# A two-layer hybrid decoder trunk on one core: scores of both attention branches in one matmul for the first two query tiles, one mask product for all heads of a step, and a new table of woven-in pieces

## What is computed

```python
def hybrid_layer(...):
    h = rmsnorm(x, g)
    z = h @ w_in
    ...
    o_cmp, p_cmp = cmp_attention(q, compress(heads(kc), pos_k, kw1, kw2), compress(heads(vc), pos_v, vw1, vw2))
    idx, ok = selection_indices(p_cmp, S)
    q_rot = apply_rope(q, cos, sin)
    o_slc = slc_attention(q_rot, apply_rope(heads(ks), cos, sin), heads(vs), idx, ok)
    o_win = win_attention(q_rot, apply_rope(heads(kwn), cos, sin), heads(vwn))
    gates = jax.nn.sigmoid(gate_logits.astype(F32)).reshape(B, S, N_HEADS, 3)
    y_nsa = (gates[..., 0:1] * o_cmp + gates[..., 1:2] * o_slc + gates[..., 2:3] * o_win).reshape(B, S, D_NSA)
    ...
    return x + y @ w_out
```

## Time and profile before

| | |
|---|---|
| median of 3 runs | 574.74 us (573.56 to 575.91) |
| the profiled execution's own time | 574.41 us |
| its span, first to last instruction | 572.6 us |
| PE busy | 547.0 us (96%) |
| DVE busy | 395.9 us (69%) |
| ACT busy | 291.9 us (51%) |
| POOL busy | 43.7 us (8%) |
| mean granted TensorE clock | 0.991 |
| bytes moved | 49.94 MB, mean 87 GB/s |

### The profile page before, as it was taken

The page is one execution under the profiler, slowest core; times in us unless marked ns, Lnnn a source line. Parts: engine busy times, 40 slices in busy tenths (PEclk is TensorE's granted clock), DMA queues, the critical chain, the costliest instruction groups (busy, mean ns, idle before and its releaser), DMA issues.

```text
span 572.6 us, 8894 instructions
## 1 busy us (share of the span) xinstructions
PE 547.0 (96%) x3327; PEld 409.8 (72%) x3327; DVE 395.9 (69%) x652; ACT 291.9 (51%) x584; POOL 43.7 (8%) x86
## 2 busy tenths in 40 slices
PE   4999999998999999999999999999899999999994
PEld 3777867777877766676887687777787777667763
DVE  4776996686866786765656679668877667676542
ACT  3647545623565554452543673562456545455431
POOL 3001100220000000000340110013000000000000
PEclk9999999998999999999999999999999999999998
DMA  9648465365111110111423756627321122000112
GB/s 260 180 146 215 114 160 107 88 135 138 38 38 38 38 37 1 38 38 38 109 76 94 182 133 164 129 62 148 98 68 38 40 73 73 1 1 2 38 37 74
DMA packets 92042, 49.94 MB, mean 87 GB/s; under 512 B 40912, under 2 KB 90208, under 8 KB 92000
## 3 DMA queue, kind: packets, MB, share of 16 engines
q1 hardware_dynamic: 89376, 45.17, 31.0%
q0 software_dynamic: 1536, 3.15, 2.3%
q10 hardware_dynamic: 1088, 1.06, 0.6%
HBM read 44.12 MB, written 2.10 MB: 81 GB/s over the span
## 4 chain that ended last, share of the span: by engine, by line
PE 80%; DVE 10%; issue 4%; ACT 3%; DMA 2%; POOL 0%; POOLq 0%; DVEq 0%; ACTq 0%
PE z_ps L1444 13%; PE z_ps L1446 12%; PE z_ps L1445 12%; PE s_ps L1516 7%; PE t_ps L1538 7%; PE o_ps L1574 5%; PE a_ps L1574 4%; PE o_ps L1444 3%; PE o_ps L1446 3%; PE o_ps L1445 3%; DVE w_lo L1072 2%; PE s_ps L1522 2%; PE t_ps L1543 1%; PE t_ps L1548 1%; PE t_ps L1635 1%
## 5 line engine op out<-in xcount | busy, mean ns | idle before, releaser
L1444 PE MATMUL z_ps<-h_hi,w_hi 128*128 128x512 f32 x248 | 102.1, 412 | 3.1 <-DVE h_lo L1056 2.3
L1008 ACT ACTIVATE probs<-s_ps,mn 128x128 f32<-128x128 f32 (+3 forms) x128 | 66.6, 523 | 74.6 <-DVE mn L1346 72.9
L1446 PE MATMUL z_ps<-h_hi,w_lo 128*128 128x512 f32 x248 | 97.8, 394 | 0.0
L1445 PE MATMUL z_ps<-h_lo,w_hi 128*128 128x512 f32 x248 | 97.8, 394 | 0.0
L866 ACT ACTIVATE w_hi<-stage 128x1024 fp32r<-128x1024 f32 x56 | 58.9, 1054 | 60.2 <-PE z_ps L1446 36.5
L1346 DVE TENSOR_REDUCE mn<-s_ps 128x1 f32<-128x384 f32 (+3 forms) x88 | 52.4, 637 | 50.2 <-PE s_ps L1522 50.0
L1072 DVE TENSOR_TENSOR w_lo<-stage,w_hi 128x1024 fp32r<-128x1024 f32 x56 | 68.4, 1221 | 10.6 <-ACT w_hi L866 9.8
L1444 PEld LDWEIGHTS z_ps<-h_hi,w_hi 128*128 128x128 f32 x248 | 47.3, 191 | 16.5 <-issue 6.6
L1446 PEld LDWEIGHTS z_ps<-h_hi,w_lo 128*128 128x128 f32 x248 | 47.1, 190 | 10.4
L1445 PEld LDWEIGHTS z_ps<-h_lo,w_hi 128*128 128x128 f32 x248 | 47.3, 191 | 8.7 <-issue 0.2
L1516 PE MATMUL s_ps<-k_st,q_st 64*128 64x128 f32 (+3 forms) x384 | 46.7, 356 | 0.2
(11 more groups left out here) (228 smaller groups left out, 915.3 us busy)
## 6 DMA issues: line engine op xcount, KB each, us to landing
stage<-in_w_in SPq DMA_DIRECT2D x28, 512.0 KB, 4.2
stage<-in_w_in SPq DMA_DIRECT2D x32, 256.0 KB, 3.8
stage<-in_cmp_k_w SPq DMA_DIRECT2D x8, 512.0 KB, 3.8
stage<-in_cmp_v_w SPq DMA_DIRECT2D x8, 512.0 KB, 5.0
stage<-in_w_out SPq DMA_DIRECT2D x8, 512.0 KB, 3.5
stage<-in_w_out SPq DMA_DIRECT2D x16, 256.0 KB, 3.9
swp<-E POOLq DMA_DIRECT2D x48, 64.0 KB, 2.3
out<-xT SPq DMA_DIRECT2D x8, 256.0 KB, 2.8
```

Of the source, the lines that this page charges most:

```text
L1008: act.activation(probs[:, 4 * pair + 2 * g + r, c0:c0 + W], s_ps[g][:, at * W:(at + 1) * W], ACT.Exp, scale=-1.0, bias=mn[:, m % 2, g, at: ...
L1444: pe.matmul(bank, w_hi[:, slot, at:at + P], x_hi, start=first, stop=False)
L1445: pe.matmul(bank, w_hi[:, slot, at:at + P], x_lo, start=False, stop=False)
L1446: ins = pe.matmul(bank, w_lo[:, slot, at:at + P], x_hi, start=False, stop=last)
```

## The change

Five edits. (1) For tiles 0 and 1 a step has the keys of both branches in one matmul: tile 0 two heads by two branches of 128 keys (twice), tile 1 one head by two branches of 256 keys (four times); before, tile 0 had four heads of one branch (twice), tile 1 two heads of one branch (four times). The number of steps stays 22 in a layer. (2) The mask is added once for all heads of a step, and its second product covers only the 64 columns that it can change. (3) The second step of tile 0 moves ahead of the rounds, with two pieces behind it. (4) The rounds of tiles 0 and 1 are put in another order (`GROUPS`, `tile_rounds`). (5) The pieces are dealt out anew, and two finished tiles `Y` keep `TILE_GAP` steps of distance.

```diff
-ROUND_PIECES = ((3,) * 9 + (2,) + (1,) * 5 + (2,) * 8 + (1,), (4,) * 9 + (3,) + (2,) * 5 + (3,) * 8 + (1,))
+ROUND_PIECES = ((3,) * 4 + (2,) * 14 + (1,) * 6, (4,) * 4 + (3,) * 12 + (2,) * 8)
+SECOND_PIECES, ROUND_AHEAD, TILE_GAP = 2, 2, 12
...
-GROUPS = [(0, 0), (0, 2), (0, 1), (1, 0), (1, 1), (1, 2), (2, 0), (2, 2), (2, 1), (3, 2), (3, 0), (3, 1)]
+GROUPS = [(0, 0), (0, 1), (0, 2), (1, 2), (1, 0), (1, 1), (2, 0), (2, 2), (2, 1), (3, 2), (3, 0), (3, 1)]
...
 def score_steps():
...
-        for b in range(2):
-            heads = [(pair, r) for pair in range(2) for r in range(2)]
-            n = (4, 2, 1, 1)[i]
-            steps += [(i, b, tuple(heads[at:at + n])) for at in range(0, 4, n)]
+        heads = [(pair, r) for pair in range(2) for r in range(2)]
+        if i < 2:
+            n = 2 - i
+            steps += [(i, (0, 1), tuple(heads[at:at + n])) for at in range(0, 4, n)]
+        else:
+            steps += [(i, (b,), (head,)) for b in range(2) for head in heads]
     return steps
...
+def parts(step):
+
+    return [(b, *head) for head in step[2] for b in step[1]]
...
+def tile_rounds():
 
     rounds = []
     for i, b in GROUPS:
...
+        if b == 2:
+            rounds.append([("C", i, pair) for pair in range(2)])
+        elif i == 0:
+            rounds += [] if b else [[("P", i, 0, pair, 0), ("P", i, 1, pair, 0)] for pair in range(2)]
+        elif i == 1:
+            rounds += [] if b else [[("P", i, c, pair, k) for k in range(2)] for pair in range(2) for c in range(2)]
+        else:
+            tiles = [("P", i, b, pair, k) for pair in range(2) for k in range(i + 1)]
+            rounds += [tiles[at:at + 2] for at in range(0, len(tiles), 2)]
+    return rounds
...
-            if waiting and silus == GROUP and waiting[0][0] <= n:
+            if waiting and silus == GROUP and max(waiting[0][0], ended_at + TILE_GAP) <= n:
+                ended_at = n
                 finish(n + 1, waiting.pop(0)[1])
...
-    s = [*fill(2), ("TURN", l, LAST), ("TURNE", l, LAST), *fill(FIRST_PIECES[l] - 2), ("CS2", l)]
-    late, needed, owed = [], [], []
+    second = ahead.pop(0)
+    s = [*fill(2), ("TURN", l, LAST), ("TURNE", l, LAST), *fill(FIRST_PIECES[l] - 2), ("S", l, second), ("MX", l, second, 0),
+         ("MX", l, second, 1), *fill(SECOND_PIECES), *exps(second), ("CS2", l)]
...
+                    before = plan.coef_no[(l, i, b)] - 1
+                    if before >= 0:
+                        l0, i0, b0 = plan.coefs[before]
+                        dve.wait_ge(t_full, turn_no[(l0, "B", i0, b0)] + 1)
...
+                many, wide = len(parts(step)), len(branches) * W
                 for at, (pair, r) in enumerate(heads):
                     q = 2 * pair + r
                     for part, (of_q, of_k) in enumerate(((0, 0), (0, 1), (1, 0))):
                         for g in range(N_KV):
                             rows = slice(g * HD, (g + 1) * HD)
...
+                            keys = k_st[rows, :, of_k, 0:W] if len(branches) == 2 else k_st[rows, branches[0], of_k, 0:W]
+                            pe.matmul(s_ps[g][:, at * wide:(at + 1) * wide], q_st[rows, GROUP * of_q + q, i * P:(i + 1) * P],
+                                      keys, start=(at == 0 and part == 0), stop=False, skip_group_check=True)
+
+                for a in range(2):
+                    for g in range(N_KV):
+                        rows = slice(g * HD, (g + 1) * HD)
+                        diagonal = s_ps[g][:, 0:many * W].rearrange("p (h w) -> p h w", h=many)[:, :, W - P + a * HD:W]
+                        later = causal_b[rows, a, a * HD:P].rearrange("p (h c) -> p h c", h=1).to_broadcast([HD, many, P - a * HD])
+                        ins = pe.matmul(diagonal, ident_b[rows, a, :], later, start=False, stop=(a == 1),
+                                  skip_group_check=True)
```

More of the change, by code:

```diff
@@ L72, in probs_before @@
 def probs_before(i, b, pair):
-    if i == 0 or (i, b) == (1, 0):
+    if i == 0:
         return []
-    if i == 1:
-        return [(0, 0, pair), (0, 1, pair)]
-    return [(1, 0, pair), (1, 1, pair)] if (i, b) == (2, 0) else [(i, 0, pair)] if b else [(i - 1, 1, pair)]
+    if i == 1 or (i, b) == (2, 0):
+        return [(i - 1, 0, pair), (i - 1, 1, pair)]
+    return [(i, 0, pair)] if b else [(i - 1, 1, pair)]
 def score_steps():
@@ L84, in score_steps, with attention @@
     for i in range(TT):
[L85 to L89 removed]
+        heads = [(pair, r) for pair in range(2) for r in range(2)]
[4 more added lines that the diff above has]
+            steps += [(i, (b,), (head,)) for b in range(2) for head in heads]
+    return steps
+def parts(step):
+    return [(b, *head) for head in step[2] for b in step[1]]
 def exp_parts(step, n):
[L94 to L95 removed]
+    if len(step[1]) == 1:
         return [(0, n)]
[L97 to L100 removed]
+    return [(at, g) for at, part in enumerate(parts(step)) if part[0] == n for g in range(N_KV)]
+def tile_rounds():
     rounds = []
     for i, b in GROUPS:
[L105 to L106 removed]
+        if b == 2:
[8 more added lines that the diff above has]
+    return rounds
+def attention(l):
+    rounds = tile_rounds()
     pieces = [("F", ("Z", l, f"gn{r}"), p) for r in range(4) for p in range(KT)]
@@ L128, in put_later @@
     def put_later(steps):
-        out, due, silus, waiting, parts = [], {}, 0, [], {}
+        out, due, silus, waiting, ready, ended, ended_at = [], {}, 0, [], {}, 0, 0
         def put(st):
@@ L184, in score @@
             return []
-        i, b, heads = ahead[0]
-        if any(turned[unit] > n for pair, _ in heads for unit in probs_before(i, b, pair)):
+        if any(turned[unit] > n for b, pair, _ in parts(ahead[0]) for unit in probs_before(ahead[0][0], b, pair)):
             return []
@@ L212, in attention @@
             s += [("S", l, step), ("MX", l, step, 0), ("MX", l, step, 1)]
-            late, needed = exps(step), [(*step[:2], pair) for pair, _ in step[2]]
+            late, needed = exps(step), [(step[0], b, pair) for b, pair, _ in parts(step)]
         s += [("W", l, tile) for tile in tiles]
@@ L390, in __init__ @@
             self.exps.append(count)
-            count += N_KV * len(key[3])
-            for pair, _ in key[3]:
-                self.exps_of[(*key[:3], pair)] = count
+            for half in range(2):
+                done = exp_parts(key[1:], half)
+                count += len(done)
+                for at, _ in done:
+                    b, pair, _ = parts(key[1:])[at]
+                    self.exps_of[(*key[:2], b, pair)] = count
         self.exps.append(count)
@@ L605, in prob_cols @@
         def prob_cols(i, b):
-            return b * P if i == 0 else (1 - b) * 2 * P if i == 1 else 0
+            return b * (i + 1) * P if i < 2 else 0
         def wait_turned(eng, key):
@@ L993, in _ @@
                     _, l, step, half = st
-                    m, (i, b, heads) = step_no[(l, *step)], step
-                    W, c0 = P * (i + 1), prob_cols(i, b)
+                    m, (i, branches, heads) = step_no[(l, *step)], step
+                    W, places = P * (i + 1), parts(step)
                     if half == 0:
@@ L1500, in scores @@
             def scores(l, step):
-                i, b, heads = step
+                i, branches, heads = step
                 m, W = step_no[(l, *step)], P * (i + 1)
```

59 lines of the change are left out of this document (27 added, 32 removed).

## The result

The changed kernel takes 565.92 us (median of 4 runs, 564.69 to 566.26); the kernel before took 575.33 us beside it (573.56 to 577.89). The ratio is 0.9838, with a 95% interval of 0.9818 to 0.9857: faster by 1.6%. The forecast was 566.5, in a range of 563.8 to 570.6. The profiled execution took 566.06 us, with a span of 564.2, so 8.35 us less than that of before.

What follows compares the result with a forecast made beforehand. PE, busy 96% of the span, was taken as the bound. Gains of 2.8, 1.1, 0.3, 1.6 and 3.6 less 1.5 us of cost gave 7.9, so 566.5 us from 574.41, in a range of 563.8 to 570.6.

Steps and rivals of the forecast that it cites:

- (c): Cost in the second step of tile 0, which splits a run of pieces: 0.1 us a layer, 0.2 in all.
- Warm steps of tile 0: Three full-clock steps of tile 0 go from 2.00 to 1.29 us by joined scores and mask, saving 2.1 us.
- The first step of layer 0: Cold step at half clock: 3.71 to 2.4 us, with 0.6 given back since the clock rises when it rises; gain 0.7.
- Tile 1: Eight steps of tile 1 go from 1.21 to 1.07 us, saving 1.1 us.
- The mask of tiles 2 and 3: Second mask product shrinks by 64 columns in 32 steps: 0 to 0.9 us, taken as 0.3, part being hidden.
- The stalls of tile 2: In layer 0, rounds 10 to 14, one more piece covers PE's short stalls: gain 1.6 us.
- the ends: Ends of both layers: 11 and 12 pieces left cover the waits, gain 3.6 us; rival that they don't gain, chance 0.08.
- (a): Cost in layer 0, rounds 18 to 22, going from two pieces to one: stalls of 0.7 us.
- (b): Cost in rounds 4 to 8, three to two pieces, if DVE is late: 0.6 us in layer 0, 0 in layer 1.
- short rounds bind everywhere: Rival: ACT or DVE late by 0.3 us in all eleven two-piece rounds up to layer 0's tile 2; 569.2 us, chance 0.14.
- The columns: Rival: joined matmuls cost by columns, so tile 0 gains only the mask; 569.0 us, chance 0.06.
- operands in runs: Slower rival: split keys and mask outputs make matmuls in tiles 0 and 1 take twice their time; 579.0 us, chance 0.07.

Runs made afterwards that it cites:

- the run without an edit: The kernel after, unaltered, run and profiled once more on the first chip; 565.37 us, ratio 0.9834.
- the table alone: Kernel before with only its table of pieces per round changed to the new one's pattern; 570.95 us, ratio 0.9909.
- the unjoined scores: Kernel after with the score matmuls of tiles 0 and 1 for each branch by itself, in the same steps; 569.01 us, ratio 0.9892.
- the old table: Kernel after with the table of pieces of the kernel before, less two in each layer for those behind the second step; 574.13 us, ratio 0.9994.

## Why the prediction was right, and where its terms were off

**The total** was 7.9 us for 8.35 measured in the profiled executions (9.4 by the medians), by terms that were off on both sides. Summed from the profile after: tile 0 4.4, tile 1 1.0, mask 0.9, tile 2 stalls 1.4, ends 3.6, less 3.2 of cost, 8.1 together, in which 0.2 of the cost, its part (c), is the forecast's own. The sum is closer than its parts are known: the first step starts at 140.00 us for 139.53, and over all profiles between 139.4 and 140.8, for reasons that lie ahead of the changed part. The reading of the waits left out one: the list of before has a third in the attention, 0.7 us ahead of a transpose, which the prediction then took among the stalls of tile 2.

**Warm steps of tile 0.** 1.24 us for the 1.29 forecast, three times: 2.3 for 2.1. Of the 0.76 a step, 0.59 are the joined scores and 0.12 the joined mask, by the steps of the two runs that undo them.

**The first step of layer 0** is the term most off. Forecast 0.7, measured 2.1: from the start of the step to the transposes behind its 18 matmuls it is 9.11 us before (139.53 to 148.64) and 7.04 after (140.00 to 147.04). Of this 0.76 is what the step gains at full clock, and 1.3 is the clock: 1.7 us of half clock in the step before, 0.55 after (1.79 for 1.24), and 5.26 us for 5.40 in the 18 matmuls (4.47 in layer 1 at full clock, with a short wait in it). The step that failed is "the clock rises when it rises": it did not rise at the old instant. But the run without an edit shows that not all of it can be the change's: of three profiles of the kernel after two have 3.4 us at half clock at this place and one none, and there the same stretch takes 5.68 us. Over all 14 profiles 6.8 us stand in three, and these are the three kernels whose first step has a matmul for each branch (before, the table alone, the unjoined scores); the eleven with joined scores have 3.4 (eight) or none (three). That speaks for a part of the change. Against it, two executions of the unjoined kernel had a mean clock of 0.997, which leaves about 3.4 us at half clock in the whole execution (an estimate: 0.003 of 565 us, doubled). How much of the 1.3 is the change's own stays open.

**Tile 1** was right in size, 1.08 for 1.07, and it doesn't come from joining the branches, which the unjoined run shows to be worth nothing there: 0.06 of the 0.13 is the joined mask, and I read the other 0.07 as the mask products that no longer stand between the heads' scores, which no run has by itself. **The mask of tiles 2 and 3** was mis-sized: the second product and the change to other work take 0.189 us for 0.215, nothing of it hidden, so 32 times 0.027 are 0.86 for 0.3, its upper bound.

**The stalls of tile 2 and the ends** were right: none of the four stalls is left, and no wait at the ends. Their sizes are 1.4 and 3.6 us, for 1.6 and 3.6: two of the four stalls stand ahead of a step, where an undelayed piece takes 0.88 us and not 0.78. The table alone, on the kernel before, gave 4.5 to 5.2 us (by medians and by ratio) where these two, less its two stalls of tile 3, make 4.4, and the old table brought the ends' waits back to a tenth. The distance between the two `Y` counts beside the table: with `TILE_GAP` at 0, 0.6 us of a stall return in this tile.

**The cost** was nearly right in layer 0 and wrong in layer 1. (a) Two stalls of 0.28, 0.56 for 0.7: a piece less shortens a round by 0.69 us, not by 0.78. (b) DVE late in two-piece rounds of layer 0: the excess of 0.21 at 172.89, 0.14 at 207.78 and 0.15 at 195.87 (1.62 us for the 1.47 of six matmuls ahead of a transpose) makes 0.5, for 0.6. For layer 1 the step said 0, since it "keeps three" pieces; it lost 1.9. What failed is that the step counted cover on PE, and neither wait was for lack of it. One is DVE's queue right behind the second step, into which the two new pieces had put an eviction ahead of `CS2`; the other is an ACT instruction that waits between two exponentials. Mending the first alone gave 0.8 back and the second 1.1, with every other piece left in its round. (c) was not measured by itself.

**The rivals.** That short rounds bind everywhere fell: most of the two-piece rounds show the undelayed 1.57 us for six matmuls. The ends gained. The columns and the operands in runs fell by their own experiments. The range held the time; but with the warm steps at their size, it held so closely because the unforeseen gain (1.4 in the first step, 0.6 of mask) and the unforeseen loss (1.9 in layer 1) nearly cancel. The mechanism of most terms was right; that the total came within 0.5 us was luck.

## What to carry to other kernels

When work is dealt out anew between steps, follow each in-order queue at every place where the count changes, not only the cover on the bound engine: a piece brings its eviction and its weight's low part along. A stall mended by taking a piece away has to be paid back at once, or all later pieces stand one place off against their operands, and the stall returns elsewhere. Repeat the profile once before reading a difference of 1 to 2 us from it; where two traces have the same order, compare them round by round from a point behind the clock's last change, which told 0.6 us here that the times did not. And price parts together: the table alone gained 4.5 us, the joined products with the old table nothing, both together 9.4.

## What the runs showed of the hardware

- At one and the same place of one program, behind a stretch in which PE was busy 1.26 of 3.40 us, the granted clock stood at half for 3.4 us or not at all; over all these kernels it was none, 3.4 or 6.8 us. Behind waits of 2.1 and 2.2 us in the middle of dense work it fell for 3.4 us in the kernel with the old table, while the kernel before, with the same wait of 2.2 us up to 559.41, stayed at full clock (its window behind the wait, the clock third from the right):

```profile
559.30:562.70 3.40, 3.29 (x17) 2.77 (x18) 0.52 (x2) 0.72 (x1) 0.54 (x1) 1.00 0.28 80
```

- A pair of score matmuls costs 0.117 us with 128 columns, 0.135 with 256 and 0.27 with 512 (three pairs of 512 take 0.81 us, 155.44 to 156.25). From 256 to 512 columns the cost goes with the columns, from 128 to 256 hardly, which is why joining two branches paid at 128 columns and not at 256. The page "TensorE: Matmul & The Clock Gate" of the Trainium skill, section "Back-to-back issue gap", gives N / 2.4 + 2.5 ns for an isolated matmul, so 0.056, 0.109 and 0.216 us for one of 128, 256 and 512 columns (estimates from that page), and says itself that at small N this counts too little where each matmul loads its weights: the pairs here take 2.1, 1.24 and 1.25 times that.
